# Half of the cached keys loaded in 32x32 blocks and turned by VectorE, with five cache buffers in place of two

## The reference, cut to what matters

```python
z = rms(x) @ w_in                               # q, k, v of both groups
fox:  s = q @ k.T / 8 + cumulated log forget    # 8 heads of 64
diff: p = softmax(q1 @ k1.T) - lam * softmax(q2 @ k2.T)   # 4 heads, k1 and k2 of 64 each
# sample: k = concat(meta k, cache_k[b] (256 rows), new k), v likewise, b = 0..7
h = x + concat(o_fox, rms(o_diff)) @ w_out
y = h + sum over 4 of 32 experts of (swiglu(rms(h) @ w_gate_up[e]) @ w_down[e]) * gate
```

## Time and profile before

| | |
|---|---|
| median of 3 runs | 1232.46 us (1232.15 to 1233.46) |
| the profiled execution, its time | 1233.77 us |
| its span, first to last instruction | 1232.0 us |
| granted TensorE clock, mean | 0.995 of full speed |
| TensorE busy | 1198.4 us, 97% |
| VectorE, ScalarE, GpSimd busy | 349.4, 195.4, 161.1 us |
| DMA | 448.66 MB in 57118 packets, mean 364 GB/s |

### The profile page before, as it was taken

How to read it: one execution, slowest core, us unless ns; L and a number is a source line. 1 busy time by engine, 2 the same in 40 slices (tenths; PEclk the granted TensorE clock), 3 DMA queues, 4 the chain that set the end, 5 groups by cost and what they waited for, 6 DMA issues and landing times.

```text
span 1232.0 us, 16177 instructions
## 1 busy us (share of the span) xinstructions
PE 1198.4 (97%) x6101; PEld 526.6 (43%) x6102; DVE 349.4 (28%) x932; ACT 195.4 (16%) x519; POOL 161.1 (13%) x382
## 2 busy tenths in 40 slices
PE   8999999999999999999999999999999999999997
PEld 4444456646434343434344443434343434243433
DVE  3234367615222121213222221212121212131313
ACT  4211366513001010101010000101010101010100
POOL 0041312101220201102020202020202011020000
PEclk9999999999999999999999999999999999999999
DMA  9613344893999999999999999999999999999995
GB/s 298 261 48 118 139 138 143 308 377 147 393 424 421 427 428 425 428 428 429 429 428 429 429 427 430 428 427 429 429 427 428 429 428 427 430 428 428 428 425 225
DMA packets 57118, 448.66 MB, mean 364 GB/s; under 512 B 10593, under 2 KB 12018, under 8 KB 31218
## 3 DMA queue, kind: packets, MB, share of 16 engines
q1 hardware_dynamic: 57032, 448.05, 88.1%
q10 hardware_dynamic: 42, 0.01, 0.0%
HBM read 442.00 MB, written 4.86 MB: 363 GB/s over the span
## 4 chain that ended last, share of the span: by engine, by line
PE 72%; DMA 22%; issue 2%; DVE 1%; SPq 1%; POOL 1%; ACT 1%; ACTq 0%; POOLq 0%; DVEq 0%
DMA arena<-in_w_gate_up 21%; PE psum L1974 21%; PE psum L2027 18%; PE psum L1696 10%; PE psum L1943 7%; PE psum L1821 3%; PE psum L2044 3%; PE psum L1988 1%; PE psum L1994 1%; DMA arena<-out_diff_v_s 1%; PE psum L1800 1%; PE psum L1732 1%; PE psum L1960 1%; PE psum L1671 1%; PE psum L2013 1%
## 5 line engine op out<-in xcount | busy, mean ns | idle before, releaser
L1974 PE MATMUL psum<-arena 128*64 128x512 f32 x2048 | 451.9, 597 | 16.5 <-DMA arena<-in_w_gate_up 16.4
L1974 PEld LDWEIGHTS psum<-arena 128*64 128x64 f32 x2048 | 148.3, 138 | 315.5 <-issue 315.2
L2027 PE MATMUL psum<-arena 128*64 128x512 f32 x992 | 216.4, 594 | 0.7
L1494 DVE TENSOR_SCALAR arena<-psum 128x256 f32<-128x256 f32 x64 | 26.8, 419 | 394.4 <-PE psum L1974 394.4
L2027 PEld LDWEIGHTS psum<-arena 128*64 128x64 f32 x992 | 75.6, 137 | 130.6 <-issue 128.9
L1696 PE MATMUL psum<-arena 128*128 128x512 f32 x288 | 129.0, 602 | 1.4 <-DVE arena L1123 1.4
L1060 ACT ACTIVATE arena<-arena 128x256 f32<-128x256 f32 x64 | 26.7, 418 | 592.0 <-DVE arena L1494 592.0
L753 POOL COPY arena<-arena 128x6 f32 (+1 forms) x16 | 3.0, 187 | 696.6 <-PE psum L2027 693.0
L2044 PE MATMUL psum<-arena 128*128 128x512 f32 x192 | 92.8, 621 | 0.0
L1943 PEld LDWEIGHTS psum<-arena 128*128 128x128 f32 x720 | 81.5, 192 | 12.2 <-issue 12.2
L1943 PE MATMUL psum<-arena 128*128 128x128 f32 x720 | 84.4, 276 | 0.0
(11 more groups left out here) (267 smaller groups left out, 794.0 us busy)
## 6 DMA issues: line engine op xcount, KB each, us to landing
arena<-in_w_gate_up SPq DMA_DIRECT2D x124, 2048.0 KB, 24.9
arena<-in_w_down SPq DMA_DIRECT2D x62, 2048.0 KB, 22.2
arena<-in_w_in SPq DMA_DIRECT2D x5, 2048.0 KB, 13.0
arena<-in_w_gate_up SPq DMA_DIRECT2D x8, 1024.0 KB, 13.6
arena<-in_cache_fox_k SPq DMA_DIRECT2D x8, 512.0 KB, 4.6
arena<-in_cache_diff_k SPq DMA_DIRECT2D x8, 512.0 KB, 5.9
arena<-in_cache_fox_v SPq DMA_DIRECT2D x8, 512.0 KB, 6.4
arena<-in_cache_diff_v SPq DMA_DIRECT2D x8, 512.0 KB, 7.6
```

Of the source, the lines that this page charges most:

```text
L1494: nc.vector.tensor_scalar(tg[n % 2], H[:, 0:512:2], 7.0, None, ALU.min).then_inc(glu_ready, 1)
L1974: last = mm(banks[n][half], XT[u][:, k, half], piece_slot(s[x])[:, c0:c0 + 512], start=(k == 0), stop=(k == 7), skip_group_check=True)
L2027: last = mm(banks[hf][half], actT[:, 4 * i + c, half], w, start=False, stop=(i == 1 and c == 3), skip_group_check=True)
```

## The change

- **Cached rows 0 to 127** of the keys of each sequence and group are loaded by four DMAs instead of one half of a DMA. Partition c of group w of 32 partitions gets runs of 32 numbers (128 bytes) out of four rows. VectorE turns them with one block transpose of 128x512 straight from the buffer into `kTc`, which takes the place of its copy. TensorE makes only the four transposes of rows 128 to 255.
- **Five cache buffers**, in ring slots 6, 7, 2, 3 and 5, sequence `b` in buffer `b % 5`, each with one semaphore that counts its 12 DMAs. `turn_cache(s)` and VectorE's `kc_evac(s)` wait for all 12, values too.
- **The order on SP**: `b` = 0 and 1 as before, 2 in the place of the first expert's weights, 3 when slot 3 is free (`maxed` 16), 4 when slot 5 is free (`mixed` 16), 5 to 7 each when the buffer's last user has been mixed. `v3` has four buffers. The first pieces of the experts' weights follow one by one, slot 3 first, slot 2 last; the residual rows `y` are loaded behind two of these pieces, where they were ahead of all three.
- **GpSimd** copies the learned rows' values into the two further `v3` buffers, in iteration 16.
- Small loads share semaphores (`s_vec`, `s_wff`, `s_small`), so their users wait for a few loads more.

```diff
-        cache = [at((12 + 2 * i) * SLOT_W, 4096).rearrange("p (s t n) -> p s t n", s=4, t=2) for i in range(2)]
+        CACHE_SLOT = (6, 7, 2, 3, 5)
+        cache = [piece_slot(s).rearrange("p (s t n) -> p s t n", s=4, t=2) for s in CACHE_SLOT]
+        CACHE_IN = 16 * 2 * (4 + 1 + 1)
...
             def load_cache(b, kv):
-                i = b % 2
+                i = b % 5
                 for g, name in enumerate(("cache_fox_", "cache_diff_")):
-                    sp.dma_start(cache[i][:, 2 * g + "kv".index(kv)],
-                                 io[name + kv][0, b].rearrange("(t p) h d -> p t (h d)", p=P)
-                                 ).then_inc((s_ck if kv == "k" else s_cv)[i], 16)
+                    rows_ = io[name + kv][0, b]
+                    if kv == "v":
+                        sp.dma_start(cache[i][:, 2 * g + 1], rows_.rearrange("(t p) h d -> p t (h d)", p=P)
+                                     ).then_inc(s_cache[i], 16)
+                        continue
+                    blocks_ = rows_[0:P].rearrange("(c k) h d -> c (k h d)", k=4).rearrange("c (m w r) -> w c m r", m=16, w=4)
+                    for w in range(4):
+                        sp.dma_start(cache[i][32 * w:32 * w + 32, 2 * g, 0].rearrange("c (m r) -> c m r", m=16),
+                                     blocks_[w]).then_inc(s_cache[i], 16)
+                    sp.dma_start(cache[i][:, 2 * g, 1], rows_[P:2 * P].rearrange("p h d -> p (h d)")
+                                 ).then_inc(s_cache[i], 16)
...
-                    elif bi not in (3, 4, 5):
-                        sp.dma_start(piece_slot(bi), piece_src(0, bi - LEAD)).then_inc(ring_in[bi], 16)
+                    elif bi == 2:
+                        load_cache(2, "k")
+                        load_cache(2, "v")
...
+            sp.wait_ge(maxed, NP)
+            load_cache(3, "k")
+            load_cache(3, "v")
+            sp.wait_ge(mixed, NP)
+            load_v3(1)
+            load_cache(4, "k")
+            load_cache(4, "v")
+            sp.wait_ge(zero_ready, 6)
+            load_v3(2)
+            load_v3(3)
+            for b in (5, 6, 7):
+                sp.wait_ge(mixed, NP + 2 * (b - 5) + 2)
+                load_v3(b - 1)
+                load_cache(b, "k")
+                load_cache(b, "v")
+            sp.wait_ge(mixed, NP + 8)
+            load_v3(7)
             sp.dma_start(before, io["before"][:, :]).then_inc(s_bef, 16)
+
+            load_piece(3)
+            sp.wait_ge(mixed, NP + 10)
+            load_piece(5)
             sp.wait_ge(kc_g, 2 * BATCH_D)
...
+            sp.wait_ge(mixed, NP + 12)
+            load_piece(6)
+            sp.wait_ge(maxed, NA - 1)
+            load_piece(4)
+            sp.wait_ge(mixed, NP + 14)
+            load_piece(7)
             sp.wait_ge(mixed, NA)
...
+            load_piece(2)
...
             def kc_evac(s):
-                ve.wait_ge(kc_T, 2 * s + 1)
+                b = s // 2
+                ve.wait_ge(s_cache[b % 5], CACHE_IN * (b // 5 + 1))
...
-                nc.vector.tensor_copy(kTc[s % 2][:, :, 0:P],
-                                      kc_bank(s, 0).rearrange("p (j r) -> p j r", j=4)).then_inc(kc_v, 1)
+                nc.vector.transpose(kTc[s % 2][:, :, 0:P].rearrange("p j (c k) -> p k j c", k=4),
+                                    cache[b % 5][:, 2 * (s % 2), 0].rearrange("p (k j r) -> p k j r", k=4, j=4)
+                                    ).then_inc(kc_v, 1)
...
             def turn_cache(s):
                 b, g = s // 2, s % 2
-                pe.wait_ge(s_ck[b % 2], 32 * (b // 2 + 1))
+                pe.wait_ge(s_cache[b % 5], CACHE_IN * (b // 5 + 1))
...
-                for t in range(2):
-                    for j in range(4):
-                        last = nc.tensor.transpose(kc_bank(s, t)[:, P * j:P * (j + 1)],
-                                                   cache[b % 2][:, 2 * g, t, P * j:P * (j + 1)], ident)
-                    last.then_inc(kc_T, 1)
+                for j in range(4):
+                    last = nc.tensor.transpose(kc_bank(s)[:, P * j:P * (j + 1)],
+                                               cache[b % 5][:, 2 * g, 1, P * j:P * (j + 1)], ident)
+                last.then_inc(kc_T, 1)
...
-                    pe.wait_ge(s_cv[b % 2], 32 * (b // 2 + 1))
-                    pe.wait_ge(s_v3[b % 2], 32 * (b // 2 + 1))
+                    pe.wait_ge(s_cache[b % 5], CACHE_IN * (b // 5 + 1))
+                    pe.wait_ge(s_v3[b % 4], 32 * (b // 4 + 1))
```

More of the change, by code:

```diff
@@ L150, in build @@
         V = at(a0 + 7296, 2048).rearrange("p (t g n) -> p t g n", t=2, g=2)
-        v3 = [at(a0 + 9344 + 1024 * i, 1024).rearrange("p (g n) -> p g n", g=2) for i in range(2)]
+        V3_AT = (a0 + 9344, a0 + 10368, a0 + 7296, a0 + 8320)
+        v3 = [at(o, 1024).rearrange("p (g n) -> p g n", g=2) for o in V3_AT]
         kTc = [at3(a0 + 11392 + 1152 * g, 4, NKEY_S) for g in range(2)]
@@ L237, in build @@
         ring_in = [sem(f"ring_in{i}") for i in range(RING)]
-        s_ck, s_cv = [sem("s_ck0"), sem("s_ck1")], [sem("s_cv0"), sem("s_cv1")]
-        s_v3 = [sem("s_v3_0"), sem("s_v3_1")]
+        s_cache = [sem(f"s_cache{i}") for i in range(5)]
+        s_v3 = [sem(f"s_v3_{i}") for i in range(4)]
         s_lfc, s_lfn, s_lfout = sem("s_lfc"), sem("s_lfn"), sem("s_lfout")
@@ L345, in build, with kc_bank @@
         copy_no = {j: n + 1 for n, j in enumerate(copies)}
-        def kc_bank(s, t):
-            return banks[(6 if s == 0 else 4) + t]
+        def kc_bank(s):
+            return banks[7 if s == 0 else 4 + s % 2]
         def scat_bank(n, last_one):
@@ L538, in _, with load_piece @@
                              ).then_inc(s_spread, 16)
-            for b in range(2, BATCH_D + 2):
-                if b < BATCH_D:
-                    sp.wait_ge(kc_T, 4 * (b - 1))
-                    load_cache(b, "k")
-                if b == 2:
-                    sp.wait_ge(mixed, NP)
-                    load_v3(1)
-                if b >= 4:
-                    sp.wait_ge(mixed, NP + 2 * (b - 4) + 2)
-                    load_cache(b - 2, "v")
-                    load_v3(b - 2)
-            sp.dma_start(before, io["before"][:, :]).then_inc(s_bef, 16)
+            sp.wait_ge(maxed, NP)
[15 more added lines that the diff above has]
+            load_v3(7)
+            sp.dma_start(before, io["before"][:, :]).then_inc(s_bef, 16)
+            def load_piece(s):
+                sp.dma_start(piece_slot(s), piece_src(0, s - LEAD)).then_inc(ring_in[s], 16)
+            load_piece(3)
+            sp.wait_ge(mixed, NP + 10)
+            load_piece(5)
             sp.wait_ge(kc_g, 2 * BATCH_D)
@@ L713, in _ @@
                     inverse_root(i - 1)
+                if i == NP:
+                    g_.wait_ge(mixed, NP)
+                    g_.wait_ge(s_v3[0], 32)
+                    for n in range(2):
+                        last = nc.gpsimd.tensor_copy(at(V3_AT[2 + n], 1024), at(V3_AT[0], 1024))
+                    last.then_inc(zero_ready, 1)
             def inverse(t):
@@ L945, in kc_evac @@
             def kc_evac(s):
-                ac.wait_ge(kc_T, 2 * s + 2)
+                ac.wait_ge(kc_T, s + 1)
                 if s == 1:
@@ L1721, in turn_cache @@
                 b, g = s // 2, s % 2
-                pe.wait_ge(s_ck[b % 2], 32 * (b // 2 + 1))
-                if s >= 1:
-                    pe.wait_ge(kc_v, s)
-                    pe.wait_ge(kc_a, s)
-                else:
+                pe.wait_ge(s_cache[b % 5], CACHE_IN * (b // 5 + 1))
+                if s >= 2:
+                    pe.wait_ge(kc_a, s - 1)
+                elif s == 0:
                     pe.wait_ge(ncs_ready, 1)
@@ L1798, in mix @@
                             vc = slice(P * j, P * (j + 1))
-                            v = cache[b % 2][:, 2 * g + 1, place, vc] if place < 2 else v3[b % 2][:, g, vc]
+                            v = cache[b % 5][:, 2 * g + 1, place, vc] if place < 2 else v3[b % 4][:, g, vc]
                             last = mm(O[32 * j:32 * j + 32, 0:P], pt[:, place, 32 * j:32 * j + 32], v,
```

42 lines of the change are left out of this document (16 added, 26 removed).

## The result

The changed kernel takes 1247.95 us, the median of 4 runs (1246.88 to 1250.74), beside 1232.7 us for the kernel before on the same chip (4 runs, 1232.15 to 1233.46). The ratio is 1.0125 with a 95% interval of 1.0111 to 1.0139: 15 us slower. I had said 1235.9 and a range to 1245.0. The direction was right, the size was not. The profiled execution took 1246.88 us, its span 1245.1, which is 13.1 more than before.

The account below looks back on a forecast made before the run. TensorE's list and the queue's bytes nearly bind the attention; four batches of 8.6 us from 202.6, plus 1.7 and a 13.05 us tail, end at 251.75, +3.4 us: 1235.9 us, own range 1233 to 1239, 8 in 10 1226.5 to 1245.

Parts of the forecast that it names:

- The place and the chain: Sample stage: batches 4 to 7 on the queue set the attention's end, which moves the kernel's end one to one.
- the sum of one batch: One sequence's loads on the queue: 4.6 us for 2 KB rows, 0.2 for `v3`, 3.8 for small packets, 8.6 us.
- B: Queue time of one sequence's cache batch, forecast 8.6 us; the kernel's change is 4B - 31.0, balanced at 7.75.
- The packets' own price: Block key loads: 4096 packets of 128 bytes a sequence at 0.92 ns each, 3.8 us.
- The dear rival: Each of eight block loads costs a 0.25 us start: B 10.6, +11.4 us, 1243.9; chance 0.14, early-stage price included.
- the price of the early stage: Small packets at 2.2 ns each, as early in the kernel: 8.9 us, B 13.7, +23.8 us, 1256.3.
- The tail: From `turn_cache(14)` to the output projection: 13.92 us before, 13.05 with two halved turns.
- The start: First DMA of sequence 4, after `mix(15)`: at 202.6 instead of 203.90, from three halved turns, 1.3 us.
- The first part of the kernel is the same: The part of the kernel ahead of the sample stage was taken as unchanged, with no cost.
- VectorE's transpose: Block transpose in place of the 692 ns copy: bounded by 0.5 and 1.4 us, taken as 0.8, covered by TensorE and queue.
- `y`, the pieces and the shared semaphores: Loads behind the attention: all hidden, 6 us to spare at the tightest; the shared semaphores' waits cost nothing.

Follow-up runs that it names:

- One wide load of such runs: Changed kernel with one DMA a group bringing 2048 runs of 128 bytes to all 128 partitions, keys partly wrong: 8.65 us a sequence, projection at 254.81.
- the plain loads: Changed kernel with each group's keys loaded by one DMA of 2 KB rows, half the sample's keys wrong: 6.0 us a sequence, projection at 243.32.
- whole rows: Changed kernel with the four block DMAs a group each bringing 32 rows of 2 KB, keys partly wrong: 7.65 us a sequence, projection at 253.00.
- wide loads: Changed kernel with four DMAs a group, each 128 columns to all 128 partitions in 512-byte packets, keys partly wrong: 7.7 us a sequence, projection at 252.97.
- the three-sequence kernel: Five cache buffers with block loads and VectorE's transpose for sequences 0 to 2 only, 3 to 7 plain: 1233.78 us, 0.9999 of the kernel before.

## Why the prediction was right in direction and wrong in size

- **The place and the chain held.** The attention's end moves the kernel's end one to one: the projection came 13.8 us later and the profiled time is 13.1 longer, the piece that waits for its last product was issued at 308.94 for 295.13, 13.8 later, and TensorE's waits for weights behind it are 15.5 us in 11 places for 16.4 in 9. The queue's four batches set the end, with the waits at s = 8, 10, 12 and 14 as named; those for `v3` are gone.
- **The step that failed is the sum of one batch.** "SP's own issuing is 14 DMAs of about 0.42 us a batch, 5.9 us, less than 8.6", and with it B = 4.6 + 0.2 + 3.8 = 8.6. The sum had the packets and nothing for the eight more DMAs. Where nothing holds it, SP's issue of a batch takes 8.6 us (7.6 for the twelve at 88 us, 1.0 for two of `v3`), not 5.9; and packets and issue don't hide each other, as a batch took 9.9 us from wait to wait, longer than either. The first took more, 12.5 us (217.32 less 203.12 and 1.7), and TensorE's wait ended 5.9 us behind the last cache issue of that batch. And SP issues four loads of `v3` behind it that were in no batch of mine, 1.8 us. From the first issue at 203.12 to `turn_cache(14)` at 247.09, less 1.7, B is 10.6 over four batches; 4 x 2.0 = 7.9 us of the 10.4 that were missing.
- **The packets' own price was nearly right.** I took 3.8 us for 4096 runs of 128 bytes. One wide load of such runs showed 2.65 over the plain loads, whose bytes (0.52 MB of 2.1) are 1.5 us: 4.1, or 3.7 without the 0.4 of its two more DMAs. By the Trainium skill ("DMA: Bandwidth & Descriptors", Why small descriptors are slow (HBM only)) it would be the 2.5 us estimated before; the measurement is 1.2 to 1.6 over that, and decides.
- **The eight DMAs cost 1.65 us** at 0.45 us of issue (whole rows). In blocks SP needs 0.63 us for each of the ten key loads. The rule that I needed is in the Trainium skill ("Perfetto Trace Analysis", What "DMA-bound" means): a queue is also bound where its issuing sequencer's track is solid. SP's track is solid here from 203.12 to 242.7, though some of its issues look held up by the full queue. How much of the 1.65 is issue and how much lies in the 16 engines wasn't told apart: with whole rows later stretches move only 260 to 300 GB/s though SP was done with its issues at 99.35.
- **The dear rival had the price.** "A start of 0.25 us" for each of eight block loads gave B = 10.6 and +11.4. B was 10.6. That is in part luck: no run shows a start of 0.25 us in the queue apart from SP's issue, and the 10.6 has the longer first batch in it. I gave this rival, with the price of the early stage, 0.14, since the row that spoke for it was one load's start on an empty queue.
- **The tail was 15.04 us, not 13.05**, the second term that was off, 2.0 us: the granted clock is 0.53 in the window behind the last wait, and five products took 1.41 us (L1790) where they took 0.84 at 203.29. I had taken the stretch at the clock before.
- **The start was 0.5 us late** (203.12 for 202.6): of the 1.3 us expected from three halved turns ahead of `mix(15)`, 0.8 came. 7.9 + 2.0 + 0.5 is the missing 10.4. That 0.8 came at all is luck of the profiled execution, which was 1.2 us earlier at its first cache load (88.12 for 89.31); from there to batch 4 it took 115.0 us for 114.6.
- **"The first part of the kernel is the same"** was wrong too, a term put at nothing: the block loads of sequence 2 ahead of the v stores cost TensorE the wait of 1.43 us at 171.28. The other kernels with block loads have it too, 0.8 to 1.5 us; those with plain keys, whole rows, wide loads or one load of runs have none.
- **VectorE's transpose** took 1.13 us, in its bounds of 0.5 to 1.4 and over the 0.8 taken. In the changed kernel its items come every 2.65 us where nothing waits, under the queue's period, so it cost nothing. Where nothing waits for the cache, from 203 to 209 us, VectorE is busy 5.79 of 6 us and TensorE waits 0.63 us for it: with the queue out of the way it would be the next to bind.
- **`y`, the pieces and the shared semaphores** cost nothing that shows, as said: `y` was issued at 252.24, ten us ahead of the projection, and TensorE waits for none of them.

## What to carry to other kernels

Before a load is cut into more DMAs, multiply their issue time as well as their bytes: on a queue that is called for, SP's count of DMAs times what one such issue takes is a bound of its own, and it is seen in the trace as a solid sequencer with a DMA share under one. It did not hide behind the engines' time here: a batch took 9.9 us, with 8.6 of issue in it. Look, too, at what stands behind the load on the same queue, as the v stores here. Price a strided load by loading that form once, not by a row of another form. A wait of some microseconds on TensorE can cost more than itself, in the clock of the stretch behind it.

## What the runs showed of the hardware that I had not expected

- One issue on SP that nothing held took 0.42 to 0.47 us for a load of up to 256 rows of 2 KB, 0.55 us for one of 2048 runs of 128 bytes, and 0.60 to 0.63 us for one of 256 or 512 runs into 32 partitions, and also for the plain second key half that stands behind those (0.62 us, where behind whole rows it is 0.42).
- Products of the same form took 0.84 us at a granted clock of 1.00 (2.4 GHz) and 1.41 us in the window with 0.53, most of it at the lower level, 1.2 GHz. TensorE had waited 4.80 us; after the wait of 2.94 us the window has 0.72, after that of 2.93 us at 236.90 it has 1.00. In the prompt attention the wait of 1.43 us left the clock at 1.00, and in the three-sequence kernel one of 1.30 us at the same place was followed by 0.64.
